# Transposing the last five row blocks of a layer inside the first part of the next block

## What is computed

```python
# end of layer 2 (i = 1)
y = y_gated @ w_out
x = layernorm(DEEPNORM_ALPHA * x + gate * y, ln_g[1], ln_b[1])
# begin of the next block (l = 0)
h = rms_norm(x, norm_mix_pre[0])
proj = h @ w_in[0]           # 1024 x 2560
q_da, k_da, v_da, q_r, k_r, v_r, g_r, u_pool = split(proj)
```

## Time and profile before

| what | value |
|---|---|
| median of 3 runs | 4088.28 us |
| lowest, highest run | 4087.81, 4091.49 us |
| the profiled execution: its own time | 4086.23 us |
| its span | 4084.4 us |
| TensorE (PE) busy, share of the span | 3870.9 us, 95% |
| VectorE (DVE) | 2204.6 us, 54% |
| ScalarE (ACT) | 1436.9 us, 35% |
| Pool (POOL) | 1908.9 us, 47% |
| chain that ended last: PE, DVE, ACT, issue | 74%, 15%, 4%, 4% |
| mean granted clock of TensorE | 0.976 of full |

### The profile page before, as it was taken

How to read it: one execution, slowest core, us unless ns; L and a number is a source line. 1 busy time by engine, 2 the same in 40 slices (tenths; PEclk the granted TensorE clock), 3 DMA queues, 4 the chain that set the end, 5 groups by cost and what they waited for, 6 DMA issues and landing times.

```text
span 4084.4 us, 49894 instructions
## 1 busy us (share of the span) xinstructions
PE 3870.9 (95%) x19191; PEld 3131.7 (77%) x19191; DVE 2204.6 (54%) x3486; ACT 1436.9 (35%) x2928; POOL 1908.9 (47%) x1709
## 2 busy tenths in 40 slices
PE   8999999989999999899898999999999898999998
PEld 4677788777888887787576788888786586788887
DVE  2242427472777775632637777624633638777633
ACT  1122223133666662222634333312222634333211
POOL 1313132362333334422234788886422135788985
PEclk9999999999999999998899999999998899999999
DMA  5312221222000002210023222453310032222543
GB/s 177 115 51 82 67 62 45 93 90 65 5 11 6 11 6 91 79 30 24 1 87 105 83 78 84 142 178 114 104 36 11 1 102 96 80 86 83 172 158 129
DMA packets 247508, 310.37 MB, mean 76 GB/s; under 512 B 38804, under 2 KB 161060, under 8 KB 247272
## 3 DMA queue, kind: packets, MB, share of 16 engines
q1 hardware_dynamic: 214456, 231.87, 18.3%
q10 hardware_dynamic: 32816, 75.32, 5.4%
HBM read 253.48 MB, written 51.53 MB: 75 GB/s over the span
## 4 chain that ended last, share of the span: by engine, by line
PE 74%; DVE 15%; ACT 4%; issue 4%; POOL 2%; DMA 1%; ACTq 0%; DVEq 0%; SPq 0%; POOLq 0%
PE ps L130 71%; PE ps L133 4%; DVE cst_sm L153 3%; DVE ml_p L142 3%; ACT thi L136 2%; DVE da_sg L159 1%; DVE tlo L142 1%; POOL wlo L142 1%; DVE f_ta L150 1%; POOL mix_z L142 1%; ACT ml_o L136 1%; DVE f_tb L150 1%; ACT tfi L136 0%; POOL whi L139 0%; DMA xin_x<-in_x 0%
## 5 line engine op out<-in xcount | busy, mean ns | idle before, releaser
L139 POOL CAST whi<-wst 128x512 fp32r<-128x512 f32 (+3 forms) x524 | 424.0, 809 | 1432.3 <-DMA wst<-in_a_w_in 453.1
L142 POOL TENSOR_TENSOR wlo<-wst,whi 128x512 fp32r<-128x512 f32 (+2 forms) x650 | 927.7, 1434 | 42.1
L130 PE MATMUL ps<-whi,thi 128*128 128x512 f32 (+3 forms) x1816 | 706.8, 389 | 9.7 <-POOL wlo L142 3.2
L130 PE MATMUL ps<-whi,tlo 128*128 128x512 f32 (+3 forms) x1816 | 686.0, 378 | 0.0
L130 PE MATMUL ps<-wlo,thi 128*128 128x512 f32 (+3 forms) x1816 | 685.6, 378 | 0.0
L130 PEld LDWEIGHTS ps<-whi,thi 128*128 128x128 f32 x1816 | 345.4, 190 | 91.8 <-issue 25.8
L130 PEld LDWEIGHTS ps<-wlo,thi 128*128 128x128 f32 x1816 | 345.3, 190 | 58.4 <-issue 3.8
L130 PEld LDWEIGHTS ps<-whi,tlo 128*128 128x128 f32 x1816 | 344.6, 190 | 57.5
L130 PE MATMUL ps<-thi,whi 128*128 128x512 f32 x856 | 338.1, 395 | 16.3 <-POOL wlo L142 11.5
L130 PE MATMUL ps<-thi,wlo 128*128 128x512 f32 x856 | 336.6, 393 | 0.0
L130 PE MATMUL ps<-tlo,whi 128*128 128x512 f32 x856 | 336.5, 393 | 0.0
(11 more groups left out here) (389 smaller groups left out, 8219.8 us busy)
## 6 DMA issues: line engine op xcount, KB each, us to landing
wst<-in_w_down SPq DMA_DIRECT2D x140, 256.0 KB, 3.3
wst<-in_w_up SPq DMA_DIRECT2D x126, 256.0 KB, 2.9
scr_h<-f_tb SPq DMA_DIRECT2D x44, 512.0 KB, 4.0
wst<-in_w_in SPq DMA_DIRECT2D x64, 256.0 KB, 2.7
wst<-in_a_w_in SPq DMA_DIRECT2D x72, 192.0 KB, 2.5
wst<-in_ada_w SPq DMA_DIRECT2D x48, 256.0 KB, 3.4
da_am<-in_ada_w SPq DMA_DIRECT2D x48, 256.0 KB, 2.6
f_T2lw<-scr_h SPq DMA_DIRECT2D x48, 256.0 KB, 3.8
```

The costliest lines, as they stand in the source:

```text
L130: return self.none if self.e is None else self.e.matmul(*a, **k)
L139: return self.none if self.e is None else self.e.tensor_copy(*a)
L142: return self.none if self.e is None else self.e.tensor_tensor(*a)
```

## The change

- Stage 5 of rows 3 and 4 leaves the row loop of layer 2 (`LATE["b"] = 3`). TensorE does the transposes of rows 3 to 7 ahead of given pieces of weights in the first part of the mix (`LAST_ROWS`: group and piece). The part's eight rows are made in groups of three, three and two.
- Pool splits pieces 3, 4 and 5 after its row 5 and pieces 6 and 7 after its row 6 (`BETWEEN`).
- ScalarE makes the high halves of rows 3, 4 and 5 before the first group's results, those of rows 6 and 7 before row 3's result; its wait for the last `mlo_hb` goes. VectorE's low halves of rows 3 to 7 are all made by `tails` after `dve_lam`.
- The layernorm's gain and offset (`lg`, `lb`) get other addresses, so that `c_rn` of rows 0 to 3 lies over nothing that is still read.

```diff
@@ layout
         z = r.new("z", [128, 8, 1024])
-        lg, lb = r.new("lg", [128, 1024]), r.new("lb", [128, 1024])
+
+        lg, lb = self.place("mlo_lg", [128, 1024], F32, gen + 61440), self.place("mlo_lb", [128, 1024], F32, mod)
+        r.off += 8192
@@ pe_tiles
-        for q in range(0, len(items), nb):
-            group = items[q:q + nb]
-            end = q + nb >= len(items)
+        sizes = nb if isinstance(nb, tuple) else (nb,) * -(-len(items) // nb)
+        for g, size in enumerate(sizes):
+            q = sum(sizes[:g])
+            group = items[q:q + size]
+            end = q + size >= len(items)
...
-                    amid(q // nb, k)
+                    amid(g, k)
@@ the row tables, rows_at, pool_out, tails
     EARLY = {"a": 2, "b": 3, "m": 3, "f": 3}
+    LATE = {"a": 5, "b": 3, "m": 5, "f": 5}
+
+    BETWEEN = {7: (3, 4, 5), 8: (6, 7)}
...
-        return [(t - n, n) for n in range(last, -1, -1) if 0 <= t - n < 8 and (n < last or t - n < 5 and st != ("f", 1))]
+        return [(t - n, n) for n in range(last, -1, -1) if 0 <= t - n < 8 and (n < last or t - n < self.LATE[self.kind(st)] and st != ("f", 1))]
...
                 self.pool_row(q, st, j, n)
+            if st == "b":
+                for k in self.BETWEEN.get(t, ()):
+                    self.split(q, ("c", 0, 3, k))
...
-    def tails(self, fn, q, st):
-        for j in range(5, 8):
+    def tails(self, fn, q, st, rows=None):
+        for j in rows or range(self.LATE[self.kind(st)], 8):
             fn(q, st, j, self.TAIL[self.kind(st)])
@@ pool_mix, pe_mix
+    LAST_ROWS = {(0, 3): 3, (0, 5): 4, (0, 7): 5, (1, 4): 6, (1, 7): 7}
+
...
-        for k in range(self.EARLY["b"], 8):
+        for k in range(self.EARLY["b"], 8) if l else ():
             self.split(q, ("c", l, 3, k))
...
-        def after(n):
-            if n == 0:
+        def after(b):
+            if l and b == 0:
                 self.tails(self.pe_row, q, prev)
 
         for n in self.PARTS:
             def amid(b, k):
+                if n == 3 and l == 0 and (b, k) in self.LAST_ROWS:
+                    self.tails(self.pe_row, q, prev, [self.LAST_ROWS[b, k]])
...
-            self.pe_tiles(q, ("c", l, n), 8, items, 4, "proj", terms, lambda k: ("c", l, n, k),
+            self.pe_tiles(q, ("c", l, n), 8, items, (3, 3, 2) if n == 3 and l == 0 else 4, "proj", terms, lambda k: ("c", l, n, k),
@@ act_mix
-        for event in self.mix_start(l):
+        for event in self.mix_start(l) if l else ():
             q.wait_ge(*event)
...
                     if n == 3:
+                        if l == 0 and j in (0, 3):
+                            self.tails(self.act_row, q, prev, [(3, 4, 5), (), (), (6, 7)][j])
+                            if j:
+                                q.wait_ge(*S.at("row_x", (prev, 7)))
                         evac(3, j, self.rn[:, j, :])
...
                 if n == 3 and b == 0:
-                    self.tails(self.act_row, q, prev)
+                    if l:
+                        self.tails(self.act_row, q, prev)
                     self.rows_stored(q, l)
```

More of the change, by code:

```diff
@@ L660, in pe_tiles @@
             if after is not None:
-                after(q // nb)
+                after(g)
     def nat(self, w, cols, act=None, out=None):
```

## The result

The changed kernel took 4098.88 us (median of nine runs, 4090.21 to 4103.21), the kernel before 4089.52 us (nine runs, 4084.42 to 4093.14). The ratio is 1.0022, with a 95% interval from 1.0013 to 1.0031: it is slower by 9.4 us, and by 5 to 13 us with the interval. The forecast was 4091.6 us in a range up to 4097, "no change" with 0.86. So the measured time lies above the range. The change is slower, clear of zero; whether by more than the 0.2% up to which the forecast said "same" is open, since the interval begins at 0.13%.

The account below looks back on a forecast made before the run. The prediction took TensorE to bound the kernel here, except for a hole at the second layer's end. It added +2.7 us for the part and 0.6 at the rotations, +3.3, to the median 4088.28: 4091.6 us, range 4087.5 to 4097.

Parts of the forecast that it names:

- Where TensorE starts: Third block's first part: after row 2's low halves (1639.8) nothing in the way, at Pool's pace to about 1657.
- Where it stops: TensorE stands still about 11.7 us before row 5's transposes, until VectorE is through with row 7 and `cst_lam`.
- the Pool term: On Pool, 9.65 + 1.0 us (one collision) moved ahead of row 7, 6.3 hidden: row 7 ends 4.35 later.
- R: Moment the bank is free and TensorE goes on with row 5's transposes: 1668.4 us from the span's start.
- rival 2: Pool held up by each of VectorE's five large operations between rows 5 and 7: +7.3 us; chance 0.08.
- From R to the end of the part: TensorE's low clock, 129 matmuls and transposes of rows 6 and 7: 34.5 us, part ends at 1702.9, +2.7 us.
- The rotations: VectorE begins to rotate at 1695.4 and has the masked scores at 1718.2; 0.6 us charged, sum +3.3 us.
- Rival 3: VectorE's rotations, slowed by splits, decide from a mean of 3.4 us a row: +13 us; chance 0.06.
- the near miss: Before the retention: VectorE's masked scores at 1718.2, needed by TensorE at about 1718.5; 0.6 us charged.
- The range: 4087.5 to 4097 us, from a little under the profiled time with +1.7 to rival 2 with 1.4 of spread.
- The bound on the gain: Last 120 matmuls come after row 3's low halves; even with row 7 not late the sum is -1.0 us.

Follow-up runs that it names:

- e1: Changed kernel with high and low halves of rows 3 to 5 back inside the row steps; seam (row 0's transposes to `rt_kz`) +1.3 us, whole 1.0005 against before.
- e3: Changed kernel with the loads and products of `cst_lam` behind the halves of rows 3 to 5; seam +4.1 us, whole 1.0015 against before.
- e5: The changed kernel run again unaltered for a second trace; seam +7.0 us, one execution of 4102.61 us.
- e4: Changed kernel with one Pool split after each of rows 4, 5 and 6 and two after row 7; seam +0.9 us, one execution of 4090.06 us.
- e9: e1 plus rows 6 and 7 transposed earlier and ScalarE taking the first group's three results before row 7's step; seam -5.9 us, whole 0.9989 against before.
- e11: Changed kernel with VectorE's `mlo_hb` of rows 3 to 7 reading one operand, a factor left out; seam +4.5 us, one execution of 4096.66 us.

## Why the prediction was wrong

- **Where TensorE starts** was right: held by row 2's low halves until 1639.77 (1639.8 expected), transposes of rows 3 and 4 without a wait. At the end of the group it waited 3.01 us for piece 6, as "at Pool's pace", and was through at 1661.0, where about 1657 was expected.
- **Where it stops** was right, in place and cause: row 5's transposes, behind VectorE's row 7 and `cst_lam`. The wait was 11.37 us (11.7 expected, 10 to 13 given as the sign), but that this length fits is luck: both its start and its end came 4 us late. e1 shows the cause by removing it, e3 shows the share of `cst_lam` (3.7 us), and the 7.4 us from Pool's row 7 to the transposes are the same in the changed kernel, in e5 and in e4.
- **The step that failed is the Pool term, "I take one such collision among all that is added, +1.0".** Five were measured, 4.9 us together, so row 7 ended at 1664.95 and not at 1661.3, and R was 1672.37 and not 1668.4 (0.35 of it is that `cst_lam`'s products took 1.30 and not 0.95). I had counted collisions in a trace where Pool's long row operations came first and VectorE had to wait. The splits are short and are put right where VectorE starts its large operations, so there it is Pool that waits. (Rows of the trace of before that show it already stand below this list.) This is rival 2, with its mechanism and nearly its price (+7.3, against +7.8 and +7.0); it was given 0.08 and should have been the forecast. The sign given for it, row 7's end after 1665, was missed by 0.05 us.
- **From R to the end of the part** was right: 34.5 us expected, and 1706.7 - 1672.4 = 34.3 measured, with the low clock charged as it was before. **The rotations** began at 1698.2 and not at 1695.4, since R was late; with the retention's first step TensorE lost 1.1 us and not 0.6. Rival 3 named a wait before `rt_it` as its sign, and one of 0.85 us is there, but it is the near miss that was priced and not rival 3's 10 us: the eight rotations took 3.0 us each on average, and rival 3 begins at 3.4.
- **The range** allowed 1.4 us for the spread of a median. The measured median is 7.3 us above the forecast: 1.2 since the kernel before came out at 4089.52 here and not at 4088.28, 4.5 at the seam (+7.8 for +3.3), and 1.5 that no run assigns. The seam costs 7.0 to 7.8 us by two traces; the measured 9.4 us (5 to 13) holds that. What the other 2 us are is not settled: they are less than the interval's half, and a single execution differs by more outside the seam.
- **The bound on the gain**, -1.0, held in each kernel that leaves the low halves where the change puts them (+0.9 in e4 is the lowest). Its reason gives 120 matmuls behind row 3's low halves, but it is 129, as the sum before it has; the -1.0 is worked out from R and does not use them. Once the low halves move it does not apply, yet e1 stopped at +1.3: a second holder of the same chain came up that I had not looked for, the result bank behind ScalarE's row 7. With that moved as well, e9 reached -5.9.

The trace of before had both orders in it. Behind row 7, two casts of splits start while VectorE writes `mlo_hb`, and both are late by 1.0: the one at 1656.89 and the one below, a third late operation that "only twice" and "Only two such cases" in the prediction leave out. The row of VectorE is the `mlo_hb` beside it. So a split that starts inside a large VectorE operation was late there too, both times.

```profile
1659.81 1.61 POOL L139 CAST whi<-wst 128x512 fp32r<-128x512 f32 x1
```

```profile
1658.69 2.26 DVE L150 SCALAR_TENSOR_TENSOR mlo_hb<-mlo_z,cst_sm,mod_sh 128x1024 f32<-128x1024 f32 x1
```

## What to carry to other kernels

When a step is moved out of one engine's loop, look on every engine for what now stands ahead of its other halves: here TensorE's transposes went early, while the copies that free their banks went behind the last row, and the hole only moved. After each such wait is removed, follow the same late event (here the end of Pool's row 7) to whatever else is queued behind it. And a collision between two engines has to be priced with the new order of their starts, and by what the first one still has to run, not with the share of collisions in the old trace.

## What the runs showed of the hardware

An operation of a split on Pool that starts during a large VectorE operation is late by the time that VectorE's operation still has to run, less 0.10 to 0.14 us. This holds for all five cases in each of three traces (changed kernel twice, e11). Beside an operation with two inputs it was 0.9 to 1.0 us, beside e11's `TENSOR_SCALAR` 0.3 to 0.5.

The same kernel had two executions 12.4 us apart, of which 1.6 us lie before the seam and -0.8 at it. Most of the rest is in two stretches where TensorE often idles: the same TensorE instructions stand 0.8 us later in the second execution at 1915 and 3.8 at 2075, 4.3 at 3120 and 10.0 at 3300. These two (the differential attention of both layers; columns as in the earlier trace rows) are of the changed kernel's first profile and of its second:

```profile
1915.00:2075.00 160.00, 133.63 (x728) 88.41 (x726) 105.44 (x192) 93.96 (x273) 38.39 (x34) 0.86 0.04 9
3120.00:3300.00 180.00, 152.91 (x825) 104.01 (x824) 110.99 (x202) 99.76 (x282) 50.99 (x45) 0.91 0.06 18
```

```profile
1915.00:2075.00 160.00, 136.38 (x705) 89.60 (x706) 105.06 (x195) 91.20 (x262) 35.99 (x30) 0.81 0.02 4
3120.00:3300.00 180.00, 155.84 (x800) 105.54 (x800) 107.19 (x198) 99.59 (x282) 41.23 (x35) 0.83 0.05 14
```

In the same stretches the granted clock was 0.86 and 0.91 in the one, 0.81 and 0.83 in the other, with the same program; less of it was done in the time (728 and 825 matmuls against 705 and 800). The kernel before had 0.87 and 0.88. How long TensorE is granted its lower level there thus differs between executions. That this makes the time, and does not only go with it, no run shows. The two profiled executions of the changed kernel lie 8.7 us below and 3.7 above its median of 4098.88. The distance between two fixed instructions around the change, which repeated to 0.8 us in two traces, was the sharper measure here: nine runs of the whole left 5 to 13 us.
